# Hidden tiles reloaded one product ahead, and another order of work around the third block's w_out and MLP, in a three-block fp32r kernel on Trainium2

## The reference

```python
def first_block(x, ...):
    ...
        h = h + mixed
        hn = rms_norm(h, norm_mlp_w[layer])
        h = h + jnp.square(jax.nn.relu(hn @ w_up[layer])) @ w_down[layer]
    out = rms_norm(h, norm_final_w)

def third_block(x, c, w_ada, b_ada, ...):
    mod = jax.nn.silu(c) @ w_ada + b_ada
    shift1, scale1, gate1, shift2, scale2, gate2 = [
        m[:, None, :] for m in jnp.split(mod, N_MOD, axis=-1)]
    ...
        h = rms_norm_3(x, norm1_pre) * (1.0 + scale1) + shift1
        z = h @ w_in
        y_a = spatial_gating(z[..., : 2 * D_A], w_spatial, b_spatial, ln_v_gain, ln_v_bias)
        y_b = multiscale_pool(z[..., 2 * D_A:], w_pool, b_pool, pool_scale)
        mix = jnp.concatenate([y_a, y_b], axis=-1) @ w_out
        x = x + gate1 * rms_norm_3(mix, norm1_post)

        h = rms_norm_3(x, norm2_pre) * (1.0 + scale2) + shift2
        f = jnp.square(jax.nn.relu(h @ w_fc1)) @ w_fc2
        x = x + gate2 * rms_norm_3(f, norm2_post)
    return x
```

## Time and profile before

| | us |
|---|---|
| median of 3 runs | 3457.92 (3457.21 to 3463.17) |
| profiled execution, its own time | 3459.79 |
| its span in the profile | 3458.0 |
| PE busy | 3361.3 |
| DVE busy | 1820.0 |
| POOL busy | 1254.0 |
| ACT busy | 1125.2 |

### The profile page before, as it was taken

How to read it: one execution, slowest core, us unless ns; L and a number is a source line. 1 busy time by engine, 2 the same in 40 slices (tenths; PEclk the granted TensorE clock), 3 DMA queues, 4 the chain that set the end, 5 groups by cost and what they waited for, 6 DMA issues and landing times.

```text
span 3458.0 us, 39464 instructions
## 1 busy us (share of the span) xinstructions
PE 3361.3 (97%) x16502; PEld 2732.0 (79%) x16502; DVE 1820.0 (53%) x2268; ACT 1125.2 (33%) x1656; POOL 1254.0 (36%) x677
## 2 busy tenths in 40 slices
PE   8999999999889999999999999999999999999998
PEld 6887888887778878775788888888887778878887
DVE  4653366555675548486455445445636475640113
ACT  5432233332121221285333222222323354442212
POOL 2212325555244213323323444444322335553543
PEclk9999999999999999999999999999999999999999
DMA  2112313235354211220111222222311132241323
GB/s 106 43 49 68 122 56 114 105 116 199 139 185 152 86 61 49 86 60 1 74 49 51 75 95 71 88 92 67 108 37 43 37 130 114 110 164 59 124 86 116
DMA packets 102749, 310.06 MB, mean 90 GB/s; under 512 B 14614, under 2 KB 21542, under 8 KB 102444
## 3 DMA queue, kind: packets, MB, share of 16 engines
q1 hardware_dynamic: 102572, 307.55, 25.4%
HBM read 255.96 MB, written 51.55 MB: 89 GB/s over the span
## 4 chain that ended last, share of the span: by engine, by line
PE 89%; DVE 5%; ACT 3%; DMA 1%; POOL 1%; issue 0%; SPq 0%; POOLq 0%; DVEq 0%; ACTq 0%
PE ps L710 22%; PE ps L711 22%; PE ps L713 22%; PE ps L767 5%; PE ps L769 5%; PE ps L768 5%; PE ps L921 1%; DVE GL L2160 1%; PE ps L1145 1%; DMA HF<-hsc 1%; POOL wlo L3125 1%; PE ps L742 1%; PE ps L744 1%; PE ps L743 1%; PE ps L1194 1%; DVE T L2160 1%
## 5 line engine op out<-in xcount | busy, mean ns | idle before, releaser
L3125 POOL TENSOR_TENSOR wlo<-raw,whi 128x1024 fp32r<-128x1024 f32 (+4 forms) x261 | 555.6, 2129 | 1410.4 <-ACT whi L1429 1410.2
L710 PE MATMUL ps<-HH,whi 128*128 128x512 f32 (+2 forms) x2240 | 891.1, 398 | 19.9 <-POOL wlo L3125 15.5
L711 PE MATMUL ps<-HL,whi 128*128 128x512 f32 (+2 forms) x2240 | 879.6, 393 | 0.0
L713 PE MATMUL ps<-HH,wlo 128*128 128x512 f32 (+2 forms) x2256 | 701.2, 392 | 0.0
L1429 ACT ACTIVATE whi<-raw 128x1024 fp32r<-128x1024 f32 (+4 forms) x261 | 237.8, 912 | 999.2 <-PE ps L713 852.2
L710 PEld LDWEIGHTS ps<-HH,whi 128*128 128x128 f32 (+2 forms) x2240 | 422.1, 188 | 114.0 <-issue 10.8
L713 PEld LDWEIGHTS ps<-HH,wlo 128*128 128x128 f32 (+2 forms) x2256 | 424.2, 188 | 94.5 <-issue 1.1
L711 PEld LDWEIGHTS ps<-HL,whi 128*128 128x128 f32 (+2 forms) x2240 | 422.0, 188 | 90.4 <-issue 2.3
L2160 DVE TENSOR_TENSOR X<-ps,X 128x1024 f32<-128x1024 f32 (+1 forms) x139 | 166.7, 1200 | 588.8 <-PE ps L713 571.6
L710 PE MATMUL ps<-GH,whi 128*128 128x512 f32 x1072 | 425.6, 397 | 22.1 <-POOL wlo L3125 21.6
L711 PE MATMUL ps<-GL,whi 128*128 128x512 f32 x1072 | 420.0, 392 | 0.0
(11 more groups left out here) (464 smaller groups left out, 4953.6 us busy)
## 6 DMA issues: line engine op xcount, KB each, us to landing
raw<-in_w_fc SPq DMA_DIRECT2D x88, 512.0 KB, 3.5
raw<-in_w_up SPq DMA_DIRECT2D x76, 512.0 KB, 3.2
raw<-in_w_in SPq DMA_DIRECT2D x70, 512.0 KB, 3.2
hsc<-T SPq DMA_DIRECT2D x50, 512.0 KB, 2.6
GF<-hsc SPq DMA_DIRECT2D x40, 512.0 KB, 5.3
T<-in_w_ada SPq DMA_DIRECT2D x32, 512.0 KB, 3.6
raw<-in_w_down SPq DMA_DIRECT2D x56, 256.0 KB, 2.7
raw<-in_w_down SPq DMA_DIRECT2D x24, 512.0 KB, 4.4
```

The lines of the kernel that those rows point to most:

```text
L710: e.matmul(o_[0:m, half(hf)], whi_[k], hi[k0 + k][:, half(hf)], start=first, stop=False)
L711: e.matmul(o_[0:m, half(hf)], whi_[k], lo[k0 + k][:, half(hf)], start=False, stop=False)
L713: i = e.matmul(o_[0:m, half(hf)], wlo_[k], hi[k0 + k][:, half(hf)], start=False, stop=last)
L3125: e.tensor_tensor(wlo_of(name), raw_of(name), whi_of(name).bitcast(F), SUB).then_inc(*po.inc("lo " + name))
```

## The change

Six things are done.

1. `ADAS` is shifted: product 0 has one row, products 1 to 8 have two, the later ones as before.
2. In both MLPs a reload is issued one product ahead: at product 0 SP issues the reloads of product 0 and 1, later at n that of n + 1 (`reload_next`). The first three row loads come behind product 0's loads. ACT and POOL make the weight of product 1 ahead of the first reloaded tile's high and low.
3. w_out3 goes by halves from wo35 on (before: from wo36). wo37's high gets a buffer of its own, WZ. The sums, the copies of the second half and the highs of fa1_2 take other places.
4. Of the gated tile, the low of piece 3 is made on DVE, and the low of piece 2 behind the product of piece 3.
5. The third MLP begins in another order: fa1_4's high right behind the root of the norm, the tiles drained as 1, 0, 2 with the fresh operands p6 and p4 ahead, fa1_5's high behind the first square, `o7h` behind `fast_hi` of the first pair.
6. In both MLPs the eight lows of the operands p4 and p7 go from DVE to POOL (`late_lows`), ahead of the first pair's lows.

```diff
-ADAS = [[2 * n, 2 * n + 1] if n < 8 else [n + 8] if n < 24 else [2 * n - 16, 2 * n - 15] if n < 32 else [] for n in range(40)]
+ADAS = [[0]] + [[2 * n - 1, 2 * n] for n in range(1, 9)] + [[n + 8] for n in range(9, 24)] + [[2 * n - 16, 2 * n - 15] for n in range(24, 32)] + [[]] * 8
...
+        WZ = at("WZ", GO + 20480, [P, 1024], R)
...
-            y3 = [po(f"y3l{k}") if k in (1, 3) else dv(f"y3l{k}") for k in range(8)]
-            for m in range(6):
+            y3 = [po("y3l1") if k == 1 else dv(f"y3l{k}") for k in range(8)]
+            for m in range(5):
...
-                if (name, hf, k) == ("wo36", 1, 4):
+                if (name, hf, k) == ("wo35", 1, 4):
                     sums_half("nm", 0, 512, dv("nm acc7 h0"))
-                elif (name, hf, k) == ("wo37", 1, 1):
+                elif (name, hf, k) == ("wo36", 1, 0):
                     spread_half("nm", 0, misc, dv("nm r1 h0"))
 
-            halves(["wo36", "wo37"], hhs, hls, lambda k, hf: [y3[k]], 8, between=mix_norm)
+            halves(["wo35", "wo36", "wo37"], hhs, hls, lambda k, hf: [y3[k]], 8, between=mix_norm)
...
                 fast_square(t, 15, 1, bias)
                 fast_square(t, 15, 0, bias)
+                highs(following(t, 1))
...
-            mixed(6, 0)
-            mixed(7, 0)
+            highs(widx["wo37"])
+            for m in (5, 6, 7):
+                mixed(m, 0)
             root_half("nm", 0, 512)
-            mixed(6, 1)
-            behind("wo36")
+            mixed(5, 1)
             highs(widx["fa1_1"])
...
-                    high(f"hh6 {k} {hf}", X[:, k, h], HH[:, k, h], either(f"x6 {k} {hf}"), pe("wo37"), scale=gains[:, 16 + k:17 + k])
+                    high(f"hh6 {k} {hf}", X[:, k, h], HH[:, k, h], either(f"x6 {k} {hf}"), pe("wo37" if hf else "wo37 h0"), scale=gains[:, 16 + k:17 + k])
                     if (k, hf) == (1, 0):
+                        mixed(6, 1)
+                    elif (k, hf) == (2, 0):
+                        highs(widx["fa1_2"])
+                    elif (k, hf) == (4, 0):
                         mixed(7, 1)
-                        highs(widx["fa1_2"])
-                    elif (k, hf) == (5, 0):
+                    elif (k, hf) == (6, 0):
                         root_half("nm", 1, 512)
...
             root_half("nx", 1, 512)
+            highs(widx["fa1_4"])
...
-                for p, tok in (("p5", f"{t}o6f {i}"), ("p6", f"{t}o7f {i}"), ("p4", f"{t}o4f {i}"), ("p7", f"{t}o7f {i}")):
+                for p, tok in (("p5", f"{t}o6f {i}"), ("p6", f"{t}o7f {i}")):
...
+            add_half("nm", 5, 0)
             add_half("nm", 6, 0)
             add_half("nm", 7, 0)
             factors_half("nm", 0)
-            add_half("nm", 6, 1)
+            add_half("nm", 5, 1)
...
                     if (n, hf) == (3, 0):
+                        add_half("nm", 6, 1)
+                    elif (n, hf) == (6, 0):
                         add_half("nm", 7, 1)
-                    elif (n, hf) == (7, 0):
+                    elif (n, hf) == (8, 0):
                         factors_half("nm", 1)
...
-                    lows(following(t, n))
+                    lows(following(t, max(1, n)))
...
+            def late_lows(t):
+
+                for p in ("p4", "p7"):
+                    for i in range(4):
+                        low(f"{t}o{p[1]}l {i}", OF[p][:, i, :], OH[p][:, i, :], OL[p][:, i, :], ac(f"{t}o{p[1]}h {i}"))
+
             lows(widx["up1"])
             lows(widx["up3"])
+            late_lows("up")
...
-            low("y3l3", UU[:, 3, :], HH[:, 3, :], HL[:, 3, :], ac("y3h3"))
...
+            late_lows("fa1_")
             fast_all("fa1_")
...
+            def reload_next(t, n):
+
+                if n < 40 and next_tile(n):
+                    f, k, to_g = next_tile(n)
+                    last = pe(f"{DN[t]}{n // 8 - 1}_7") if n > 7 else last_tx(t) if k in (2, 3) else pe(f"{t}15 p3")
+                    reload(t, f, k, 1 - to_g, pe(f"{t}15 p3"), last)
+
             def down(t, n):
 
-                if next_tile(n):
-                    f, k, to_g = next_tile(n)
-                    reload(t, f, k, 1 - to_g, pe(f"{t}15 p3"), last_tx(t), *([pe(f"{DN[t]}{n // 8 - 1}_7")] if n > 7 else []))
+                if n == 0:
+                    reload_next(t, 0)
+                reload_next(t, n + 1)
                 behind("{}{}_{}".format(DN[t], *divmod(n, 8)))
...
-            for f in range(3):
-                row_load(f)
...
                 down("up", n)
+                if n == 0:
+                    for f in range(3):
+                        row_load(f)
```

More of the change, by code:

```diff
@@ L441, in build @@
         cidx = {name: i for i, name in enumerate(cut)}
-        ring = [name for name in cut if name not in ("fa1_1", "fa1_3", "fa2_4_7") and name not in SPLIT]
+        ring = [name for name in cut if name not in ("wo37", "fa1_1", "fa1_3", "fa2_4_7") and name not in SPLIT]
         ridx = {name: i for i, name in enumerate(ring)}
@@ L464, in whi_of @@
                 return HH[:, 0:2, half(1)]
-            return (WX if name == "fa1_1" else WY if name == "fa1_3" else whi[ridx[name] % 2])[:, 0:n]
+            return (WX if name == "fa1_1" else WY if name == "fa1_3" else WZ if name == "wo37" else whi[ridx[name] % 2])[:, 0:n]
         def wlo_of(name):
@@ L1416, in highs @@
                         q.wait_ge(*dv("zu3"))
-                    elif name == "fa1_3":
+                    elif name in ("wo37", "fa1_3"):
                         q.wait_ge(*pe("sp3"))
@@ L2025, in scalar @@
                 gelu(f"zu{m}", UU[:, m, :], pbias[:, m:m + 1])
-            for k in (1, 2):
-                high(f"y3h{k}", UU[:, k, :], HH[:, k, :], dv(f"uu{k}"))
+            high("y3h1", UU[:, 1, :], HH[:, 1, :], dv("uu1"))
             behind("zu3")
+            high("y3h2", UU[:, 2, :], HH[:, 2, :], dv("uu2"))
             high("y3h3", UU[:, 3, :], HH[:, 3, :], dv("uu3"))
@@ L2110, in fa1_square @@
                 e.activation(T[f % 3][:], T[f % 3][:], ACT.Square).then_inc(*ac.inc(f"fa1_s{f}"))
-            for f in range(3):
-                relu(f)
-                fa1_square(f)
-                high(f"fa1_o5h {f}", OF["p5"][:, f, :], OH["p5"][:, f, :])
-            high("fa1_o5h 3", OF["p5"][:, 3, :], OH["p5"][:, 3, :])
-            highs(widx["fa1_4"])
+            for i in range(4):
+                high(f"fa1_o5h {i}", OF["p5"][:, i, :], OH["p5"][:, i, :], ac(f"fa1_o5f {i}"))
+            relu(1)
+            fa1_square(1)
+            highs(widx["fa1_5"])
+            relu(0)
+            fa1_square(0)
             for i in range(4):
                 high(f"fa1_o6h {i}", OF["p6"][:, i, :], OH["p6"][:, i, :], dv(f"fa1_o6f {i}"))
+            relu(2)
+            fa1_square(2)
+            for i in range(4):
+                high(f"fa1_o4h {i}", OF["p4"][:, i, :], OH["p4"][:, i, :], dv(f"fa1_o4f {i}"))
             relu(3)
             fa1_square(3)
-            highs(widx["fa1_5"])
-            for i in range(4):
-                high(f"fa1_o4h {i}", OF["p4"][:, i, :], OH["p4"][:, i, :], dv(f"fa1_o4f {i}"))
-            relu(4)
-            fa1_square(4)
             for w in range(2):
@@ L2943, in spatial @@
                 if m == 3:
-                    for k in (0, 2):
-                        q.wait_ge(*ac(f"y3h{k}"))
-                        tt(HL[:, k, :], UU[:, k, :], HH[:, k, :].bitcast(F), SUB, f"y3l{k}")
+                    y3_low(0)
                 q.wait_ge(*ac(f"zu{m}"))
@@ L3041, in vector @@
                 fresh("p6", i)
+            for i in range(4):
+                fresh("p4", i)
             q.wait_ge(*ac("nx rt"))
-            for f in range(3):
+            for f in (1, 0, 2):
                 drain("fa1_", f, True)
@@ L3047, in vector @@
             for i in range(4):
-                fresh("p4", i)
-            drain("fa1_", 3, True)
-            for i in range(4):
                 fresh("p7", i)
                 fresh_low("p6", i)
+            drain("fa1_", 3, True)
+            fast_sums("fa1_", 3)
             drain("fa1_", 4, True)
-            for i in range(4):
-                fresh_low("p4", i)
-            fast_sums("fa1_", 3)
             drain("fa1_", 5, True)
-            for i in range(4):
-                fresh_low("p7", i)
             fast_all("fa1_", True)
```

24 lines of the change are left out of this document (15 added, 9 removed).

## The result

The changed kernel takes 3438.28 us in the median of 4 runs (3437.67 to 3443.38); the kernel before, 3459.0 beside it (3457.21 to 3463.17). The ratio is 0.9942, with a 95% interval from 0.9924 to 0.9959. The gain is 20.7 us. Forecast were 51, and 3438 lies above the range of 3392 to 3428. The sign was right, the size was not.

The account below looks back on a forecast made before the run. TensorE, busy in 97% of the span, was taken as the bound; only its waits and the lower clock after them could give. 30.3 + 10.6 + 10.4 − 0.5 = 50.8 us, forecast 3407 us, own range 3398 to 3416, wider range 3392 to 3428.

Parts of the forecast that it names:

- A: First block's down products, reloads one product ahead: 34.4 us at stake in waits and clock, gain 30.3.
- the port's term: Port shared by VectorE and GpSimd: 6.65 us per reloading product against TensorE's 5.7; 4.1 us of waits left.
- the rival that had got 0.13: Port binds in every reloading product, 7.9 us each from 8 to 23: time 3428; chance 0.13.
- Products 8 to 15: First block's down products: row waits of 1.3, 0.4, 0.4 and 0.1 at this group's entry, together 2.2 us.
- Four lows before "up": Operand lows moved to POOL before the first MLP's first part: cost 0 to 1.5 us, taken as 0.5.
- B: Gated tile, w_out3 and begin of the third MLP: gain 10.6 us, bounds 0 and 20.
- Gated tile: Wait of 3.1 us behind POOL's low: 1.0 left, for the third piece, gain 2.1.
- fa1_2: Third MLP's begin: its weight low still 3.0 us late, the sum of the norm at fa1_0 3.3 late.
- First pair: Third MLP's first pair, part p1: a wait of 3.2 us behind POOL's operand lows, bounds 0.6 and 10.6.
- Clock: Lower clock after waits, gated tile to third MLP: of 5.2 us, half, 2.5, left as loss.
- C: Third MLP's first reload: 7.8 us of waits and 2.6 of clock go, gain 10.4.
- the fifth rival: Short row waits at each product keep TensorE's clock at 1.2 GHz: 3488 us, slower than before; chance 0.02.

Follow-up runs that it names:

- the run with all five edits: Changed kernel; products 8-23's tile lows on VectorE; rows 0, 1 loaded first; fa1_2's high, wo37's copy earlier; third MLP's p7 lows later; first MLP's lows on VectorE: 3403.35 us.
- the run with six: The run with all five edits, with the tile lows of products 0 to 3 on VectorE too; ratio 0.9854 to the kernel before.

## Why the prediction was wrong, and where it was right

**What was at stake in A was sized rightly**: 34.4 us, and the kernel that takes the tile lows off GpSimd and loads rows 0 and 1 first gets 31.9. Wrong was the claim that the change alone gets 30.3: it got 2.9, since 23.6 us of waits and 7.2 of clock were left where the prediction had 4.1 and none.

**The failed step is the port's term.** The prediction saw that row work and lows add up (6.65 us a product), took a lag of 0.95 us for each of eight products, and subtracted a whole product of slack: 1.9 us left for products 16 to 23. Measured were four waits of 4.2, 2.3, 3.5 and 4.5 us, 14.5 in all, and 5 us of clock. Two things were wrong. A product costs 7.6 us, not 6.65: GpSimd's four lows of two products fall into one row, and behind the other row VectorE is idle for 2.0 to 3.6 us, since its next sum waits for TensorE's product, which was held up by the row before. A rate made of busy times alone leaves such idle time out. And the slack of 5.7 us, on which the forecast let the lag pile up before TensorE would feel it, does not exist: VectorE can't begin a row before its product ends and its sum is made, so each row has 4.5 us, and what it takes beyond them is a wait at once (4.2, 2.2, 3.4 and 4.5 by the table above, against the measured 4.2, 2.3, 3.5 and 4.5). The 7.6 us are near the price (7.9) of the rival that had got 0.13. It was right to count the sum into X into each product's chain, though not by its reason: nothing held the sum up, which took 1.21 to 1.23 us throughout. (The Trainium skill, "SBUF — State Buffer", section "Who interferes with whom", says that a VectorE instruction with at most one input in SBUF, outside the two-port modes, does not contend with GpSimd; the trace agrees.)

Products 8 to 15 were nearly right (2.9 us of waits against 2.2).

**The second failed step is row 0.** The row loads were moved behind two reloads, and the prediction gave that nothing: it counted the wait removed and not the queue that the row load was moved behind. Forecast 0, measured 6.2 and 2.2 of clock. Some 2.7 us of the wait are the late load and some 3.5 the stretched operations, an estimate from the chain above. The run with rows 0 and 1 loaded first shows what the order cost: there the row runs free before the lows begin, and the wait at row 0 is gone.

**Four lows before "up"**: 0.5 against 1.7. The prediction spoke of four and counted eight, and counted them at 1.32 us; they took 1.74, and the wait came not behind GpSimd but behind a drain of VectorE (1.4 us).

**B came out at 8.3 instead of 10.6, near the forecast partly by luck: errors in it cancel.**
- Gated tile: left 1.0, measured 1.0. Right.
- fa1_2: its low was forecast 3.0 us late, the sum of the norm 3.3. What came first was the PSUM tile, which no step had looked at: 7.7 us. It covered both: with the copy earlier a wait of 4.3 for the low appeared, and with that gone one of 1.6 for the sum.
- First pair: 3.2 against 4.2, behind the low of p1 as said; the run with p7's lows later shows that these set it.
- Clock: 2.5 against 1.6 + 1.6 = 3.2.

**C was right**: both orders were turned, and all of it went, 10.9 us.

The slowdown of the fifth rival, a granted clock that stays low from short waits on rows, did not come: A has nine such waits, and only those of 3.5 us and more are followed by 0.64 or 0.72. But short waits are not harmless in every place. With fa1_2's high earlier, two waits on the copies, of 1.0 and 1.2 us with 1 us of work between them, were followed by 0.72 (the window below begins behind the second). The same two waits (1.1 and 1.2 us) in the run with all five edits were too, and those of 0.7 and 1.2 us in the run with six were not.

```profile
2737.35:2743.35 6.00, 6.00 (x19) 0.72 0.00 1
```

The Trainium skill, "TensorE: Matmul & The Clock Gate", section "A second HAM failure mode: psum-queue depth-cycling", says that TensorE's clock goes up and down when the engine idles for short times often enough. Those two runs agree; the rows in A show none of it.

VectorE's seven multiply-adds took 2.68 us alone and 5.68 to 8.69 beside GpSimd. The Trainium skill's rule on the shared pair, in the section named above, agrees with that.

**What stays open:** what reloads in even order would be worth by themselves, since the one run that tried it also made the rows late; why A differs by up to 3.1 us between executions that no edit reaches; and whether the other parts of the changed order in B would be worth more in another combination.

## What to carry to other kernels

When a wait is removed, work out the rate of what comes next, each engine's work and what it stands still for in one period, and compare it with the bottleneck's period. Subtract slack only if the late engine can work ahead with it: here VectorE could not begin a row before its product ended, so each row had its own 4.5 us and nothing carried over. Subtractions on GpSimd are not free beside a busy VectorE: where VectorE would do the piece in half the time, giving it back can be faster for both. And with each instruction that is moved, look at what it frees (here a PSUM tile) and at what it is now queued behind (here row 0's load).

## What the runs showed of the hardware

- The conflict slows both sides: 128x512 subtractions on GpSimd took 1.74 us instead of 1.3 beside VectorE's work, and VectorE's rows (eight 128x128 operations each) up to 9.0 us instead of 3.0.
- A 512 KB load landed 3.2 to 3.4 us after its issue when none was issued shortly before it, 6.8 us when it stood behind two reloads and a weight issued in the 1.9 us before it, and 9.5 us as the last of six within 2.8 us.
- Behind the same wait of 7.7 us on the copy the granted clock of the next 6 us was 0.73, 0.75 and 0.52 in three runs (changed kernel, rows first, p7's lows later): the same wait costs 1.5 to 2.9 us of clock.
- The first 210 us, which no edit touches, differed by up to 9 us between executions: the granted clock was 0.97 in both of the windows to 100 and 210 us in one run, and 0.94 and 0.99 in another. A difference of a few microseconds between whole runs is no evidence here. Between the same two instructions it can be: C came out the same within 0.1 us, but A, with its many waits, only within 3.1.

```profile
0.00:100.00 100.00, 88.20 (x474) 0.97 0.29 102
100.00:210.00 110.00, 108.79 (x802) 0.97 0.12 44
...
0.00:100.00 100.00, 82.96 (x402) 0.94 0.27 96
100.00:210.00 110.00, 108.79 (x852) 0.99 0.14 49
```

(Windows of PE in the run of all five edits, and in that with six.)
